# A two-layer hybrid decoder on eight cores: lambdas after the first norm, x in pairs of chunks, the merge in groups of four chunks, the last mixer and the last FFN output tile by tile

## The reference, cut to what matters

```python
D_MODEL, BATCH, SEQ, DEPTH = 1024, 8, 2048, 2       # d_ff = 2816
for l in range(DEPTH):
    h = rmsnorm(x, norm_mix_pre[l])
    z = h @ w_in[l]                                   # -> u, v | q | k | v | pool | 3 gates
    ya = gmlp_branch(gelu(za), ...)                   # chunks of 128 tokens, causal, 4 groups x 128
    yb = diff_attention(zq, zk, zv, lambdas..., ...)  # 4 heads, q and k 2 x 64, v 128, causal
    yc = pool_branch(zc, ...)                         # windows 2, 4, 8, 16
    up = einsum('bsnw,nwd->bsnd', stack([ya, yb, yc]), w_branch[l])
    merged = sum(sigmoid(zg) * up)                    # three gated branches, each 1024 wide
    x = x + rmsnorm(merged @ w_out[l], norm_mix_post[l])
    h = rmsnorm(x, norm_ffn_pre[l])
    g, u = split(h @ w_ffn_in[l])
    x = x + rmsnorm((silu(g) * u) @ w_ffn_out[l], norm_ffn_post[l])

# differential attention, per head and block of 128 queries:
lam = exp(sum(lq1 * lk1)) - exp(sum(lq2 * lk2)) + lambda_init
w = softmax(q1 k1^T) - lam * softmax(q2 k2^T)
out = rmsnorm(w @ v, subln_g) * (1 - lambda_init)
```

## Time and profile before

| what | value |
|---|---|
| runs shown | 2547.53, 2549.86, 2853.38 us, median 2549.86 |
| the profiled execution, its own time | 2544.49 us |
| its span on the slowest core (core 2) | 2542.9 us |
| spans of the eight cores | 2530.6 to 2542.9 us |
| mean granted TensorE clock | 0.962 to 0.967 |
| PE busy | 2278.0 us (90%) |
| DVE, ACT, POOL busy | 1456.8, 1265.8, 288.9 us |
| DMA | 227.79 MB, mean 90 GB/s |

### The profile page before, as it was taken

The page is one execution under the profiler, slowest core; times in us unless marked ns, Lnnn a source line. Parts: engine busy times, 40 slices in busy tenths (PEclk is TensorE's granted clock), DMA queues, the critical chain, the costliest instruction groups (busy, mean ns, idle before and its releaser), DMA issues.

```text
span 2542.9 us, 39515 instructions; the slowest of 8 cores (2530.6 to 2542.9 us)
## 1 busy us (share of the span) xinstructions
PE 2278.0 (90%) x12331; PEld 1077.9 (42%) x12568; DVE 1456.8 (57%) x2619; ACT 1265.8 (50%) x2719; POOL 288.9 (11%) x567
## 2 busy tenths in 40 slices
PE   2999679999998997999999999999999798969994
PEld 0444334444453443444444444444444344424441
DVE  2366645577656885555534754567856688354312
ACT  2446636456566664634446442656567466341121
POOL 0111100001111100001011110001011111000010
PEclk9999879999998997999999999999999899989998
DMA  6533536533356544664446547633335534544487
GB/s 147 110 38 51 104 42 130 88 57 55 47 70 136 81 56 104 112 117 64 65 58 113 116 71 152 146 67 57 53 52 92 131 51 68 119 120 77 76 121 170
DMA packets 89161, 227.79 MB, mean 90 GB/s; under 512 B 8704, under 2 KB 9472, under 8 KB 88960
## 3 DMA queue, kind: packets, MB, share of 16 engines
q0 software_dynamic: 48592, 147.35, 39.2%
q1 hardware_dynamic: 40368, 77.91, 10.8%
HBM read 339.00 MB, written 33.55 MB: 147 GB/s over the span
## 4 chain that ended last, share of the span: by engine, by line
PE 81%; DMA 5%; ACT 5%; DVE 4%; issue 4%; SPq 1%; POOL 0%; ACTq 0%; DVEq 0%; POOLq 0%
PE ps L1012 58%; PE ps L1053 11%; PE ps L1171 3%; DMA WS<-wblk 3%; PE ps L1200 2%; PE ps L1103 2%; PE ps L1185 2%; DVE st L1480 1%; DMA TG<-lam 1%; ACT WT L1253 1%; DVE R L1387 1%; PE ps L1175 1%; ACT PB L1314 1%; DMA XR<-xm 1%; DVE R L1390 1%
## 5 line engine op out<-in xcount | busy, mean ns | idle before, releaser
L1012 PE MATMUL ps<-HB,WS 128*128 128x512 bf16 x4981 | 1155.8, 381 | 18.4 <-DVE HB L1390 3.1
L1012 PEld LDWEIGHTS ps<-HB,WS 128*128 128x128 bf16 x5120 | 492.5, 98 | 593.9 <-issue 41.0
L1253 ACT ACTIVATE TG<-ps 128x512 f32<-128x512 f32 x368 | 219.6, 597 | 537.5 <-PE ps L1012 535.6
L1480 DVE TENSOR_REDUCE st<-ps 128x1 f32<-128x1024 f32 (+7 forms) x384 | 343.3, 908 | 168.8 <-PE ps L1175 155.4
L1314 ACT ACTIVATE PB<-ps,st 128x1024 bf16<-128x1024 f32 (+7 forms) x384 | 331.3, 865 | 144.9 <-DVE st L1480 126.9
L887 POOL DMA_DIRECT2D WS<-wblk x328 | 178.2, 543 | 1878.0 <-PE ps L1012 1513.9
L1390 DVE SCALAR_TENSOR_TENSOR TM<-TG,ps 128x512 f32<-128x512 f32 x304 | 208.7, 686 | 288.7 <-ACT TG L1253 150.7
L1053 PE MATMUL ps<-R,WS 128*128 128x512 bf16 x1369 | 317.9, 382 | 14.6 <-DMA WS<-wblk 9.6
L1253 ACT ACTIVATE R<-ps 128x512 f32<-128x512 f32 (+1 forms) x256 | 149.5, 596 | 252.3 <-PE ps L1053 125.7
L1012 PE MATMUL ps<-R,WS 128*128 128x512 bf16 x994 | 239.1, 379 | 3.0 <-ACT TG L1253 0.7
L1053 PEld LDWEIGHTS ps<-R,WS 128*128 128x128 bf16 x1408 | 133.9, 98 | 172.4 <-issue 29.1
(11 more groups left out here) (87 smaller groups left out, 1686.3 us busy)
## 6 DMA issues: line engine op xcount, KB each, us to landing
WS<-wblk POOLq DMA_DIRECT2D x184, 512.0 KB, 6.0
WS<-wblk POOLq DMA_DIRECT2D x80, 352.0 KB, 5.4
xm<-R SPq DMA_DIRECT2D x8, 2048.0 KB, 9.2
XR<-xm SPq DMA_DIRECT2D x64, 256.0 KB, 8.1
WS<-wblk POOLq DMA_DIRECT2D x32, 384.0 KB, 6.1
R<-xT SPq DMA_DIRECT2D x32, 256.0 KB, 6.7
WS<-wblk POOLq DMA_DIRECT2D x32, 256.0 KB, 7.0
x<-R SPq DMA_DIRECT2D x4, 2048.0 KB, 12.3
```

The lines of the kernel that those rows point to most:

```text
L1012: mm = e.matmul(bank(b), lh, rh, start=i == 0, stop=i == len(pairs) - 1)
L1253: e.activation(out=out, in_=in_, func=func, scale=scale, bias=bias).then_inc(*inc(sem, key))
L1480: e.tensor_reduce(out=col(2 if c else 0), in_=src, axis=AX.X, op=ALU.max, negate=True).then_inc(*inc("dve_max", (s, u, c, comp, "m") if c ...
```

## The change

- **Lambdas.** They are still loaded behind x, but DVE multiplies and sums them just ahead of the first row maximum, ACT exponentiates ahead of its first exp, and DVE finishes ahead of its first w. The load of the gMLP norm's constants (gbc) on SP still waits for the sums.
- **x two chunks a transfer.** x, both scratch tensors and the output lie in DRAM as [tile, partition, chunk, token]; a first x transfer and a last output transfer carry two chunks (512 KB). The whole-tile store and the residual load become one contiguous run of each partition. POOL's later weight loads wait for the third pair of tile 0 instead of the eighth chunk.
- **Merge.** In stages 0 to 2 four chunks of tile 0, then the same four of tile 1, and so for the other four. finish_attention moves behind the first four groups, which count as dense progress; the total given to attention grows by 4 * 12 matmuls, the reserve stays 24.
- **Last mixer.** Stage 3 does the 8 chunks of tile 0, out_proj of tile 0, the 8 chunks of tile 1, out_proj of tile 1; blocks C and out are loaded once for each tile.
- **Last FFN.** ffn_in takes j = 0 to 3 for tile 0, then for tile 1, then as before. ffn_out takes output chunks 0 to 2 for both tiles with one load, and chunks 3 to 7 tile by tile.
- **Norm factor in PSUM.** The factor after a mixer (kind "o") lies in PSUM bank 0 or 1, two of the banks of the attention scores, instead of TM. The first QK^T of stages 1 to 3 therefore waits for h of both tiles, and the first rs for the last exp.
- **pv.** The planner takes the next query block's first pv only when y is there in its model, and takes other steps until then.

```diff
+RESERVE = 24.0
...
-                elif last:
-                    self.op("sp", ("out", s, t, oc), 0.1, 1, [("xn", kind, s, t, oc, n)], mb=0.25)
+                elif last and oc % 2:
+                    self.op("sp", ("out", s, t, oc), 0.1, 1, [("xn", kind, s, t, oc, n)], mb=0.5)
...
     def attention_step(self):
         a = self.att
-        if a["pv"] and self.there([a["pv"][0][0]], None):
+        if a["pv"] and self.there(self.pv_needs(), None):
...
+        if s and u == 0:
+            needs += [("h", "o", s - 1, t, 7) for t in range(2)]
...
+    def pv_needs(self):
+        need, u, r, nb, last, rnd = self.att["pv"][0]
+        return [need] + ([("y", self.att["s"], u // 4 - 1)] if u % 4 == 0 and r == 0 and u else [])
...
     def ffn_in(self, s):
-        for j in range(22):
-            for t in range(2):
+        first = 4 if s == 4 else 0
+        for j, t in [(j, t) for t in range(2) for j in range(first)] + [(j, t) for j in range(first, 22) for t in range(2)]:
...
     def ffn_out(self, s):
-        order = [(oc, t) for oc in range(8) for t in range(2)] if s < 4 else [(oc, t) for t in range(2) for oc in range(8)]
+        both = 8 if s < 4 else 3
+        order = [(oc, t) for oc in range(both) for t in range(2)] + [(oc, t) for t in range(2) for oc in range(both, 8)]
...
+    def fout_block(self, s, oc, p, t):
+        return (s, "fout", oc, p, t) if s == 4 and oc >= 3 else (s, "fout", oc, p)
...
-        for dc in range(8):
-            for t in range(2):
-                i = self.gating
...
+        if s == 3:
+            order = [(dc, t) for t in range(2) for dc in range(8)]
+        else:
+            order = [(4 * g + k, t) for g in range(2) for t in range(2) for k in range(4)]
+        for n, (dc, t) in enumerate(order):
+            if n == 4:
+                self.finish_attention()
+                self.paused = True
+            if s == 3 and n == 8:
+                self.out_proj(s, 0)
+            block = self.pass_of(s, "C", dc, t)
...
+    def pass_of(self, s, what, i, t):
+        return (s, what, i, t) if s == 3 else (s, what, i)
+
+    def out_proj(self, s, t):
+        for oc in range(8):
...
-            x = self.op("sp", ("x0", half, t, oc), 0.1, 0 if half == 0 else 3, before, mb=0.25)
+            if oc % 2 == 0:
+                x = self.op("sp", ("x0", half, t, oc // 2), 0.1, 0 if half == 0 else 3, before, mb=0.5)
...
-            self.attention(s, ffn + 16 * 24 * self.MM)
+            self.attention(s, ffn + (16 * 24 + 4 * 12) * self.MM)
...
             self.gates(s)
-            self.paused = True
-            self.finish_attention()
             self.merge(s)
-            self.out_proj(s)
+            if s < 3:
+                self.out_proj(s, 0)
+            self.out_proj(s, 1)
...
-    xTd = dt_in("xT", [D, S_LEN])
+    xTd = dt_in("xT", [4, 128, 8, 512])
...
+    def over_rms(kind, t):
+        return bank(t) if kind == "o" else TM[:, t, :]
...
-                g.wait_ge(*ev("X07", 0))
+                g.wait_ge(*ev("X02", 0))
...
-            if n == 15:
+            if n == 7:
                 for l in range(2):
                     e.dma_start(out=lamb[:, l, :], in_=lamd[l:l + 1, :].partition_broadcast(128)).then_inc(*inc(f"LAM{l}", 0, 16))
...
+            if s:
+                pe.wait_ge(*ev("dve_h", ("o", s - 1, 0, 7)))
+                pe.wait_ge(*ev("dve_h", ("o", s - 1, 1, 7)))
...
             if kind == "o" and which == "p":
-                a.wait_ge(*ev("dve_mc", (s, 7, 1)))
-            run("act_rs", (kind, s, t, which, "ln"), TM[:, t, :], bank(C.bank[key]), AF.Ln, 1.0 / D, EPS)
+                a.wait_ge(*ev("act_exp", (s, 31, len(key_chunks(STAGES[s][1], 7)) - 1, 1)))
+            if kind == "o" and which == "x":
+                a.wait_ge(*ev("dve_xn", (kind, s, t, 7)))
+            run("act_rs", (kind, s, t, which, "ln"), over_rms(kind, t), bank(C.bank[key]), AF.Ln, 1.0 / D, EPS)
...
-        a.wait_ge(*ev("dve_lam", (1, "s2")))
-        run("act_lam", 0, lamc[:, :, 4:6], lamc[:, :, 2:4], AF.Exp)
         a.wait_ge(*ev("dve_const", "sub"))
+        first = True
         for name, *args in order["act"]:
+            if name == "exp" and first:
+                first = False
+                a.wait_ge(*ev("dve_lam", (1, "s2")))
+                run("act_lam", 0, lamc[:, :, 4:6], lamc[:, :, 2:4], AF.Exp)
             work[name](*args)
...
-        lambdas()
-        neg_lambda()
         done = 0
         for name, *args in order["dve"]:
             if name == "max" and done == 0:
+                lambdas()
                 spatial(0)
                 done = 1
+            if name == "w" and done == 1:
+                neg_lambda()
+                done = 2
```

More of the change, by code:

```diff
@@ L410, in attention @@
         for x in w:
-            targets.append((total - 24.0) * cum / sum(w))
+            targets.append((total - RESERVE) * cum / sum(w))
             cum += x
@@ L1043, in ffn_out @@
         def ffn_out(s, oc, t, part):
[L1044 removed]
+            block = plan.fout_block(s, oc, part, t)
             loaded(block)
```

104 lines of the change are left out of this document (54 added, 50 removed).

## The result

The kernel after takes 2516.86 us (median of 4 executions, 2513.92 to 2526.1) against a median of 2547.53 for the kernel before on the same chip. Their ratio is 0.9886, 95% interval [0.9865, 0.9906]: 29 us or 1.1% less. I had forecast 2482 with a range of 2444 to 2512; the time is outside it, on the slow side. What follows was measured with changed kernels. Medians and ratios leave out executions in which one die ran slower than the other at a lower clock, stretches come from the cores of one such even die (die 0; die 1 for m_n0_early, n_reload and o_best_pv_old), and a run without a ratio had too few executions left for one.

A forecast was written before the change was run, and what follows sets the result against it. The prediction took the kernel as bound by PE's matmuls outside the clock dips, with gains only in the dips. Its terms summed to -66 us from 2544.5, 2478.5, put at a median of 2482 us, range 2444 to 2512.

The forecast's parts named there:

- start: Before K's first matmul: without the wait for the lambdas K starts at about 30 to 31 us, -24 us.
- stage 0: groups in front: Stage 0's merge: 48 matmuls put ahead take 16 us and shorten the drain by 20, winning 14 us.
- stage 0: PV rule: Stage 0's attention: the planner fills part of PE's 17.1 us of waits for YB, winning 4 us.
- stage 1, groups and rule: Stage 1: dense groups ahead of the attention's rest win 7 us and the YB waits 1, -8 us.
- stage 3's groups in front: Stage 3's drain: 10.4 us of dense work put into its 13.9 us, -8 us.
- weights: Merges: blocks used up faster or loaded twice cost 2 us in stage 2 and 8 in stage 3, +10 us.
- tile by tile inside stage 3's merge: Stage 3's merge: tile 0's norm on DVE fits beside tile 1's merge and out_proj, at no cost.
- last mixer to last FFN: Between last mixer and last FFN: lost time falls from 26.7 to 15 us, -11 us.
- last FFN's output: Last FFN's output: 26 loads instead of 32 leave 13 of 20 us lost, -7 us.
- Rival 2: Stage 3 to the end: DMA becomes the bound, weights cost 25 us, last output wins 2; 2508 us, chance 0.20.
- rival 3: Start: x, not the lambdas, holds it, as early weight loads push tile 1 to 40 us; 2495, chance 0.05.
- Rival 4: Attention: the held-back first pv queues behind dense groups, 74 us more drain; 2556 us, chance 0.04.

The follow-up runs named there:

- m_n0_early: i with the rest of the attention finished before the first merge group and the residual loaded from the last gate; mean span 2479.6 us against 2459.3.
- n_reload: i with stage 3's C and out blocks loaded once for each tile, in the shared order; 2486.78 us, ratio 0.9755.
- o_best_pv_old: i with the planner's old rule for the first PV of a query block; 2498.94 us, ratio 0.9797.
- d: Kernel before with only the lambdas' work moved, to the first row maximum and first exp; 2526.1 us, ratio 0.9935.
- b_gate_x11: Kernel after with POOL's second to fourth weight loads held until the second pair of x tile 1 has landed; 2505.21 us, ratio 0.9849.
- l_pv_only: Kernel before with only the planner's new rule for the first PV of a query block; 2523.47 us, ratio 0.9927.
- a: Kernel after with each stage's residual load waiting for the fourth merge group instead of the last gate; 2496.08 us, ratio 0.9811.
- e: Kernel after with b_gate_x11's load gate, late residual in stages 0, 1 and 3, old merge order in stage 2; mean span 2473.5 us.
- i: e with stage 3 back to shared blocks, as in f; 2473.6 us, ratio 0.9729.
- f: Kernel after with stage 3 in the merge order of stages 0 to 2, then both output projections; stage 3 and FFN 834.4 us against 842.0.
- k_first0: Kernel after with the last FFN's input in its old order, without four pairs of tile 0 first; 2514.72 us, ratio 0.9896.
- h: Kernel after with the last FFN's output in its old order, 32 loads; that stretch 91.0 us against 82.6.
- c_n0: Kernel after with the rest of the attention finished ahead of the first merge group; 2512.96 us, ratio 0.9895.
- j_best_n0: i with the attention finished ahead of the first merge group, residual still behind the fourth; mean span 2508.8 us.

## Why the prediction failed

By its own steps, forecast against what the runs isolate:

| step | forecast | in the kernel after | alone, or without the collision |
|---|---|---|---|
| start | -24 | -18.8 | -18.7 lambdas (d); -27 with the loads held (b) |
| x in pairs | 0 | 0 at the start | 0 at the start (d); beside the weights not tested |
| stage 0: groups in front | -14 | +2.1 | -6.4 to -7.4 (m, o) |
| stage 0: PV rule | -4 | -4.1 | -13.0 (l), -13.1 (o) |
| stage 1, groups and rule | -8 | +3.2 | -4.9 (m) and -2.0 (l) |
| stage 3's groups in front | -8 | +1.0 | -6.7 (m) |
| weights | +10 | +24 to +29 | residual 18 to 23 (a), order in stage 2 6 (e, i) |
| tile by tile inside stage 3's merge | 0 | +6 | +6 of the 7.6 (f) |
| last mixer to last FFN | -11 | -5 | pairs -3.5 (k), tile by tile 0 (f) |
| last FFN's output | -7 | -9.9 | -8.4 (h) |

**The step that failed is "Weights".** It put "2 in stage 2, 8 in stage 3" and nothing in stages 0 and 1, where "drains give it slack". It saw the residual only in stage 3's sum of demands. The four groups had been moved to the very place where SP issues 4 MB, and the slack lies *behind* them: 0.86 of DMA beside the groups, 0.00 in the drain. In stages 0, 1 and 3 that cost 8.0, 9.0 and 6.4 us on die 0. In stage 2 the step named the right thing, the third and fourth block come late, but at 1 to 2 us each: on core 0 PE waits 2.06 and 2.14 us for them and goes on at half the clock, and the order costs 6. The 8 us of stall in stage 3 did not come: PE waits 2.4 us for weights in that merge, all of it in the first four groups. Together 24 to 29 us of direct cost where I had 10; that is 14 to 19 of the 35 us that the forecast missed.

Rival 2 (2508 us) comes nearest in number, but not in its reasons: it had DMA as the bound at the end of stage 3 and a last output that wins 2 us, and the runs show no wait for weights behind the fourth group of stage 3 at a DMA share of 0.89, and 8 to 10 us won at the output.

**Tile by tile in stage 3** had a term at nothing. I took tile 0's norm as hidden beside tile 1's merge, since DVE's "18 us need about 31, and fit". DVE then needed 2.85 us a group, so PE went at DVE's pace; with the late start of tile 0's output projection some 6 us were lost.

**The start** failed as rival 3 described it, with about half its price (8.1 us of 14, b_gate_x11): tile 1 was pushed, to 32.5 us and not to 40. I read the drop from 330 to 187 GB/s as the end of x and took 23 us for tile 1 in a kernel that issues weights before that. 5 of the missed us.

**The drains.** The sum for stage 0 came out near the truth for the wrong parts, and that is luck: without the collision it is 19.5 us, forecast 18, but 13 of it is the PV rule, which I had put at 4 of the 17.1 us of YB waits, and 6.5 the groups, which I had put at 14. Those 14 rested on a drain shorter by 20 us; between c_n0 and the kernel after it shrinks by 11.5. Why dense work brings the attention forward by less than the 5.3 us a unit of the earlier trace rows is not shown; that stretch also held waits for YB, which are gone now. The drains, which I had at 36, 23 and under 6 us, are 42.4, 24.8 and 5.8. Rival 4, the held-back PV as a loss, is refuted by l_pv_only.

**Last mixer to last FFN** was mis-sized by 6. I set 26.7 us lost before against 15 after, but the 26.7 are idle time and slow clock together and the 15 idle time alone. Like for like, PE is idle for 35.4 - 15.1 = 20.3 us before and was to be idle for 15; in the kernel after it waits 18.4. What little is won comes from the four pairs (3.5, k_first0), for the shared order has 13.8 us of tile 1's output projection beside tile 0's norm anyway, and waits as long.

**Slips in the sums**, too small to matter: 2549.9 - 66 is 2484 and not 2482, and in stage 1 14 us beside dense work bring 0.82 unit forward and not 0.87.

**Right:** that the last output is won by fewer loads (26 in place of 32; forecast 7, 8.4 us isolated), that the pairs change nothing at the start, and that the residual's bytes and the weights' share engines: the Trainium skill, "DMA: Bandwidth & Descriptors" (Issuing engines are not separate DMA queues), says that transfers of SP and POOL run on the same 16 engines and interleave. The trace agrees: in the 8 us from 265 us on both queues moved, 118 and 111 packets, and the 384 KB block beside a 4 MB residual took 16 us, where a block of that size has a median of 5.6. I used the page for stage 3 and the last output alone, and not where the change put the two side by side. The 2 us of fixed cost that the prediction took from the same page of the Trainium skill stand there, under "Anatomy of one DMA", for transfers issued by GpSimd, and x is issued by SP, so the rows of x do not test that figure.

## What to carry to other kernels

Work that is moved to fill an idle stretch is moved next to other transfers: read the DMA share of the place it goes to, not of the place as a whole, and look for a bulk load issued at the same event; let the bulk load wait until the engine that needs weights is idle anyway (one wait moved was worth 19 us). Look at the size of the packets of either queue too: beside 16 KB packets the weights came at half the rate that they had beside 2 KB ones, though what that cost here was not isolated. A wait removed elsewhere can be eaten by such a stall, so a part measured inside the changed kernel can show a third of its worth (4.1 of 13.1 us); measure it in the kernel before as well. An order that uses up a new block in half the time (2.59 in place of 5.18 us) needs its loads twice as fast for that while: count what else is under way just then. And work hidden on a helper engine stays hidden only if the helper, with both tasks, needs less time a group than the engine that waits for it (here 2.85 us against 2.59).

## What was not expected of the hardware

A small transfer on one queue, issued just behind a large one on another, hardly passed it: 384 KB landed 16.0 us after their issue beside 4 MB at 228 to 282 GB/s (kernel after), and 15.4 us in j_best_n0; the median of such a block in the kernel after is 5.6. The queues moved nearly as many packets, 118 and 111 in 8 us, but of 16 KB and under 3 KB. The factor in PSUM changed nothing on DVE: a norm's scalar_tensor_tensor with it takes 742 ns, with the factor in SBUF 741, so that neither my -1 us came about nor the +1 us that I estimated from the Trainium skill, "VectorE: DVE Perf Modes" (The TRN2 errata). Two groups of DVE by shape, busy us and mean ns:

```profile
L1425 DVE SCALAR_TENSOR_TENSOR R<-R,cols_s,ps 128x512 f32<-128x512 f32 x64 | 47.5, 742 | 73.8 <-ACT ps L1283 73.8
L1425 DVE SCALAR_TENSOR_TENSOR R<-R,cols_s,TM 128x512 f32<-128x512 f32 x64 | 47.4, 741 | 85.9 <-ACT TM L1283 85.9
```

What stays open: how much of the collision the 16 KB packets make, since neither the old layout nor a finer splitting of the residual was tried with the new merge; what the doubled loads of stage 3 cost by themselves; and why stage 2 grew by 4 to 5 us with the old PV rule.
